# Handing a quarter of the last output columns to GpSimd, and storing them with VectorE's in one DMA

## The reference, cut to what matters

```python
def _rmsnorm(x, g):
    r = lax.rsqrt(jnp.mean(xf * xf, axis=-1, keepdims=True) + EPS)
    return (xf * r).astype(x.dtype) * g

def reference(...):                       # DEPTH = 1, SEQ = 256, D_MODEL = 2048
    h = _rmsnorm(x, norm_mix[0])
    ...                                   # gated convolution and pool group, both into y
    x = x + y @ w_out[0]
    h = _rmsnorm(x, norm_mlp[0])
    u = jax.nn.relu(h @ w_up[0])
    x = x + (u * u) @ w_down[0]
    return _rmsnorm(x, norm_final)
```

## Time and profile before

| | us |
|---|---|
| median of 3 runs | 949.27 |
| lowest and highest of them | 949.05, 949.37 |
| the profiled execution, its own time | 949.0 |
| span of the profiled execution, first to last instruction | 947.1 |
| PE busy | 938.6 (99%) |
| DVE busy | 772.1 (82%) |
| ACT busy | 549.4 (58%) |
| POOL busy | 59.6 (6%) |

### The profile page before, as it was taken

One profiled execution on the slowest core, in us unless ns is written; L12 is line 12 of the kernel. 1 busy time (PEld: TensorE's weight loads), 2 busy tenths in 40 slices (PEclk: granted clock), 3 DMA queues, 4 the chain that ended last, 5 costly groups with the idle time before them and its releaser, 6 DMA issues.

```text
span 947.1 us, 11968 instructions
## 1 busy us (share of the span) xinstructions
PE 938.6 (99%) x4880; PEld 807.9 (85%) x4880; DVE 772.1 (82%) x646; ACT 549.4 (58%) x445; POOL 59.6 (6%) x76
## 2 busy tenths in 40 slices
PE   9999999999999999999999999999999999999997
PEld 8888888888888888888888888888888888888885
DVE  6697766987866798798788879878887987888797
ACT  7744345655744666575575557557555755755555
POOL 0000000100000101010000101000010100001000
PEclk9999999999999999999999999999999999999999
DMA  9966452899966999999999999999999999999972
GB/s 332 410 237 226 170 200 100 253 277 286 273 235 239 274 283 335 332 293 347 282 305 291 306 350 269 328 283 312 301 301 355 262 323 285 309 295 303 333 213 91
DMA packets 39508, 265.12 MB, mean 280 GB/s; under 512 B 4384, under 2 KB 4768, under 8 KB 8224
## 3 DMA queue, kind: packets, MB, share of 16 engines
q1 hardware_dynamic: 29232, 191.62, 50.7%
q0 software_dynamic: 9792, 71.31, 38.0%
q10 hardware_dynamic: 432, 1.46, 0.4%
HBM read 262.28 MB, written 2.10 MB: 279 GB/s over the span
## 4 chain that ended last, share of the span: by engine, by line
PE 99%; DMA 0%; DVE 0%; ACT 0%; DVEq 0%; issue 0%; ACTq 0%
PE ps L522 37%; PE ps L525 19%; PE ps L775 10%; PE ps L773 10%; PE ps L779 10%; PE ps L685 3%; PE ps L691 2%; PE ps L818 2%; PE ps L666 1%; PE ps L664 1%; PE ps L670 1%; PE ps L825 1%; DMA first<-params 0%; PE ps L547 0%; PE ps L592 0%; PE ps L546 0%
## 5 line engine op out<-in xcount | busy, mean ns | idle before, releaser
L522 PE MATMUL ps<-act_a,w_hi 128*128 128x512 f32 x1536 | 367.3, 390 | 0.4 <-DVE act_a L1268 0.4
L1467 DVE TENSOR_TENSOR w_lo<-w_raw,w_hi 128x2048 fp32r<-128x2048 f32 x144 | 328.9, 2287 | 7.6 <-ACT w_hi L982 6.3
L522 PEld LDWEIGHTS ps<-act_a,w_hi 128*128 128x128 f32 x1536 | 285.0, 188 | 57.6 <-DVE act_a L1268 0.7
L982 ACT ACTIVATE w_hi<-w_raw 128x2048 fp32r<-128x2048 f32 x144 | 274.7, 1913 | 83.7 <-PE ps L779 42.7
L525 PEld LDWEIGHTS ps<-act_a,w_lo 128*128 128x128 f32 x1536 | 198.4, 191 | 8.4
L525 PE MATMUL ps<-act_a,w_lo 128*128 128x256 f32 x1536 | 201.3, 283 | 0.0
L982 ACT ACTIVATE w_hi<-mix_mem 128x2048 fp32r<-128x2048 f32 x51 | 97.6, 1913 | 116.1 <-PE ps L525 94.8
L775 PE MATMUL ps<-w_hi,act_b 128*128 128x512 f32 x420 | 164.2, 391 | 0.0
L773 PE MATMUL ps<-w_hi,act_b 128*128 128x512 f32 x420 | 164.0, 390 | 0.0
L1467 DVE TENSOR_TENSOR w_lo<-mix_mem,w_hi 128x2048 fp32r<-128x2048 f32 x51 | 116.8, 2291 | 55.5 <-ACT w_hi L982 55.1
L779 PE MATMUL ps<-w_lo,act_b 128*128 128x512 f32 x420 | 112.2, 389 | 0.0
(11 more groups left out here) (126 smaller groups left out, 547.0 us busy)
## 6 DMA issues: line engine op xcount, KB each, us to landing
w_raw<-w_stream SPq DMA_DIRECT2D x106, 1024.0 KB, 8.5
w_raw<-w_quads SPq DMA_DIRECT2D x49, 1024.0 KB, 9.1
mix_mem<-w_quads POOLq DMA_DIRECT2D x45, 1024.0 KB, 11.4
mix_mem<-w_quads SPq DMA_DIRECT2D x15, 1024.0 KB, 7.7
w_raw<-w_quads POOLq DMA_DIRECT2D x15, 1024.0 KB, 11.3
mix_mem<-w_stream POOLq DMA_DIRECT2D x6, 1024.0 KB, 9.1
w_raw<-w_stream SPq DMA_DIRECT2D x16, 256.0 KB, 6.9
x<-x_rows SPq DMA_DIRECT2D x2, 1024.0 KB, 17.5
```

The lines of the kernel that those rows point to most:

```text
L522: return pe.matmul(ps[:, bank, :], weights_hi, act, start=first, stop=False)
L982: act.activation(w_hi[:, g % 4, :], raw, ACT.Copy).then_inc(hi_ready, inc)
L1467: dve.tensor_tensor(out=w_lo[:, g % 4, :], in0=raw, in1=w_hi[:, g % 4, :].bitcast(F32), op=ALU.subtract).then_inc(lo_ready, inc)
```

## The change

Block 1 of the second token half (columns 512 to 1023) and block 0 (columns 0 to 511) are divided anew. ACT scales columns 0 to 255 of the two blocks, POOL scales columns 256 to 767 with a tensor_scalar in place, and DVE scales columns 768 to 1023. The columns 512 to 767 therefore need their gain beforehand, so that DVE's times_g of this half is 768 columns wide. ACT stores columns 0 to 255 (128 KB); SP stores columns 256 to 1023 (384 KB) in one DMA, for which it waits for DVE and for POOL. The number of stores stays seven.

```diff
+PART_ACT, PART_POOL = 256, 768
...
+        out_by_pool = sem("out_by_pool")
...
             sp.wait_ge(out_by_dve, 4)
-            store(1, 1)
+            sp.wait_ge(out_by_pool, 1)
+            sp.dma_start(out[:, 1, PART_ACT:2 * BLOCK_COLS], x[:, 1, PART_ACT:2 * BLOCK_COLS])\
+              .then_inc(out_stored, 16)
             sp.wait_ge(out_stored, 16 * (HALVES * OUT_BLOCKS - 1))
...
+            pool.wait_ge(x_times_g, 3)
+            pool.wait_ge(r_ready, 4)
+            rows = x[:, 1, PART_ACT:PART_POOL]
+            pool.tensor_scalar(rows, rows, r_tok[:, 1:2], None, op0=ALU.mult).then_inc(out_by_pool, 1)
...
                 for j in (2, 0):
-                    xj = x[:, t, BLOCK_COLS * j:BLOCK_COLS * (j + 1)]
+                    last = t == 1 and j == 0
+                    xj = x[:, t, BLOCK_COLS * j:PART_ACT if last else BLOCK_COLS * (j + 1)]
                     act.activation(xj, xj, ACT.Copy, scale=r_tok[:, t:t + 1]).then_inc(out_by_act, 1)
...
-            act.dma_start(out[:, 1, 0:BLOCK_COLS], x[:, 1, 0:BLOCK_COLS])\
+            act.dma_start(out[:, 1, 0:PART_ACT], x[:, 1, 0:PART_ACT])\
...
-            def times_g(j, t0, t1, squares):
+            def times_g(j, t0, t1, squares, width=BLOCK_COLS):
...
             def scale(t, j):
                 cols = slice(BLOCK_COLS * j, BLOCK_COLS * (j + 1))
-                dve.scalar_tensor_tensor(out=x[:, t, cols], in0=rows_of(t, j),
+                of = rows_of(t, j)
+                if t == 1 and j == 1:
+                    cols = slice(PART_POOL, 2 * BLOCK_COLS)
+                    of = x[:, t, cols]
+                dve.scalar_tensor_tensor(out=x[:, t, cols], in0=of,
...
-            times_g(0, 1, HALVES, 7)
+            times_g(0, 1, HALVES, 7, PART_POOL)
```

More of the change, by code:

```diff
@@ L1701, in _ @@
             before = HALVES * (1 + OUT_BLOCKS)
-            def times_g(j, t0, t1, squares):
+            def times_g(j, t0, t1, squares, width=BLOCK_COLS):
                 dve.wait_ge(ssq_ready, before + squares)
-                xj = x[:, t0:t1, BLOCK_COLS * j:BLOCK_COLS * (j + 1)]
-                gj = g_row[:, None, BLOCK_COLS * j:BLOCK_COLS * (j + 1)]\
-                    .to_broadcast([P, t1 - t0, BLOCK_COLS])
+                xj = x[:, t0:t1, BLOCK_COLS * j:BLOCK_COLS * j + width]
+                gj = g_row[:, None, BLOCK_COLS * j:BLOCK_COLS * j + width]\
+                    .to_broadcast([P, t1 - t0, width])
                 dve.tensor_tensor(out=xj, in0=xj, in1=gj, op=ALU.mult).then_inc(x_times_g, 1)
```

## The result

The changed kernel takes 951.17 us (median of 15 runs, 950.65 to 951.75) against 949.27 us (15 runs, 948.6 to 949.81). The ratio is 1.002, with a 95% interval of 1.0014 to 1.0027. That is 1.9 us more. The forecast was 949.25 us, no change.

What follows compares the result with a forecast made beforehand. PE is busy 99% of the span; the 5.2 us tail is bound by the first store's issue and full DMA engines. Earlier issues win only 0.04 us, nothing, so 949.25 us, unchanged; range 948.85 to 949.75.

Steps and rivals of the forecast that it cites:

- the forecast's first sum: Tail: first store issued 942.71, 0.79 us to bytes, 2.8 us for 1 MiB, 0.8 us to span end 947.1.
- Nothing is queued behind it: POOL's new tensor_scalar: starts about 941.95 with nothing behind it in POOL's queue; last earlier work a DMA issue at 913.69.
- POOL may take 2.4 us before it costs anything: POOL's cover before SP's last store: issue may come as late as 944.4, 1.3 us after DVE's end.
- the signs that the forecast named for being wrong: Profile after: DMA gap between stores, POOL over 2.4 us, DVE's first scaling above 0.75, r_tok over 1.8 behind PE.
- The rival on the slower side: Late POOL delays SP's last store; over 0.2% (1.9 us) slower only from 4.4 us, 951.2 or more; chance 0.03.
- Its fetch: POOL's first tensor_scalar might have to fetch something; only a fetch of over 3 us gives 951.2 or more.
- The product's 0.27 us: DVE's times_g, 256 columns wider: 0.27 us longer, fits 0.31 us idle before the next instruction with 0.05 to spare.
- ACT's and DVE's halved scalings: Second scalings at 256 columns: ACT about 0.22 us less, ending 943.01; DVE 481 ns against 745, ending 943.05.
- last issue earlier by 0.2 us: SP's joint 384 KB store issued at 943.08 instead of 943.34, its time to landing longer by as much.
- 0.53 us forecast by the memsets: POOL's 512-column tensor_scalar, priced by memset rows: 98 ns plus 0.83 ns a column; POOL ends at 942.5.
- the far end of 1.5: Upper size of POOL's tensor_scalar, twice DVE's 512-column scaling: 1.5 us, POOL ending at 943.45.
- The lock: Rival: DVE's scalings and POOL can't run together; near end hidden, far end 949.4; chance 0.10 shared with late POOL.

Runs made afterwards that it cites:

- a bare wait on r_tok: The kernel before, with POOL only waiting for the last r_tok before its end, without an instruction: 949.49 us against 949.11, ratio 1.0006.
- the run with the early drain: The changed kernel with one more POOL drain ahead of its two last waits: 949.09 us against 948.84, ratio 1.0001.
- The early tensor_scalar: The kernel before with a one-column POOL tensor_scalar right after its last DMA issue: 949.13 us against 949.09, ratio 1.0.

## Why the prediction was wrong, step by step

**The step that failed** is the last term of the forecast's first sum, "0.8 us to the end of the span (947.1)". It took the end of the span as the last landing plus a constant. It is a meeting of all engines, and the end is the later of two sums: last landing + 0.4 us, and POOL's last instruction + 5.3 us + 0.25 us. Before, POOL's drain was over at 925.2. The change put its sum at 943.85 + 5.3 + 0.25 = 949.4, 2.0 us behind the first, 943.94 + 3.1 + 0.4 = 947.4 (issue and landing of the last store). With it failed the sentences "Nothing is queued behind it" on POOL's new instruction, since the drain was, and "POOL may take 2.4 us before it costs anything": its true cover was negative, as even a bare wait on r_tok made POOL 0.5 us late.

None of the signs that the forecast named for being wrong appeared: no gap between the stores, POOL's row 1.57 us and not over 2.4, DVE's first scaling 0.75 us as before, r_tok 1.83 us behind PE's last matmul in both kernels. All four look at what comes ahead of the last landing, and the loss lay behind it.

**The rival on the slower side** put the threshold for 951.2 us at a POOL instruction of 4.4 us, through the last store. The time was met, the mechanism wasn't: with 1.57 us of POOL work the store was still hidden. So that rival names another cause for the same number, and that 951.2 us was met is a coincidence. Its fetch did not show either: POOL's row began 0.19 us after r_tok was ready, and the two configuration instructions had run at 914.4.

**What held.** The DMA engines are full from the first store's bytes to the last, and the two later issues don't set the end: the last issue came 0.4 us later after r_tok than before, and without POOL's drain the time was the same within the interval. The product's 0.27 us were covered, with the 0.05 us to spare that was forecast. ACT's and DVE's halved scalings are as computed (1.12 us for ACT's two, 0.47 us for DVE's). The forecast had the last issue earlier by 0.2 us; POOL made it later by 0.4, and the full DMA engines hid that. The run with DVE in POOL's place, 949.11 us, is the forecast of everything but POOL.

**What was mis-sized.** POOL's tensor_scalar: 0.53 us forecast by the memsets, 1.57 us measured, a little past the far end of 1.5. The Trainium skill's "GPSIMD Engine Reference", section "Elementwise — side-by-side cycle accounting", from which the forecast estimated 0.44 us, does not agree with this row either. The difference of 1.0 us is in the result, since the drain moves one for one with this instruction. It also began 0.19 us after r_tok and not 0.08. The bare wait costs 0.5 us in the trace, the instruction 1.57 us: together the 2.1 us of the tail, near the 1.9 us of the medians. So with 0.53 us for the instruction the kernel would still have lost some 1 us, and the missing drain, not this size, is what the forecast had wrong.

**The lock.** DVE's second scaling reads two tensors from SBUF and started at 942.79 while POOL read SBUF from 942.28 to 943.85. It took 0.47 us and was not held up. The Trainium skill's "SBUF — State Buffer", section "Who interferes with whom", would have the second to come wait for the whole of the first; here it did not. Whether POOL lost some time to DVE was not tried. Its rows leave room for it: a straight line through 0.61 us for 128 columns and 0.84 us for 256 (with a constant) gives an estimate of 1.30 us for 512, where 1.57 us were measured.

## What to carry to other kernels

Before giving an idle engine a last piece of work, look at what its queue still holds behind it, the drain at the end included, and when every engine reaches the final barrier; an engine that ends early hides a price that appears once it ends late. On POOL that price was about 0.08 us for each DMA of 1 MB that it had issued since its last drain, up to the 68 of this kernel; an extra drain in idle time, or a block that ends without it once all transfers have been waited for, takes it off. And when the tail is one full stretch of the DMA engines, helping with the scaling of later pieces buys nothing.

## What the runs showed of the hardware that I had not expected

- POOL's drain: 0.16 us with no DMA issued by POOL, 0.25 with 1, 1.49 with 16, 5.74 with 68, but 2.06 with 136, which fits the 23 DMAs behind a pause of 7.49 us in POOL's issuing. In the kernel studied 5.3 us for 68.
- POOL's tensor_scalar in place, with a scalar per partition: 0.61 us for 128 columns, 0.84 for 256 with a constant, 1.57 for 512. DVE's tensor_scalar of the same 512 columns took 0.48 us, less than its 0.75 us for 512 columns with two tensors.
- A tensor_scalar brings two configuration instructions into POOL's queue, 0.36 us each in the changed kernel and 11 ns in the run with the early drain, where they came right behind that drain. The early tensor_scalar shows that they cost nothing at the end.
